# A two-layer block on one core: modulation tiles in pairs at the start, inputs 0 to 511 first, and pooling matmuls one chunk later

## The chip, the cores and the metric

The kernel runs on one core of a Trainium2 chip. The time is the device time of one execution, in microseconds (us); three runs of the kernel before gave 3119.91 to 3122.59, median 3122.0. One more execution was profiled, and all rows below are of that one.

Engine names as in the profile: PE is TensorE (PEld its weight loads), DVE VectorE, ACT ScalarE, POOL GpSimd, SP the engine that here issues every DMA, in order.

## The reference

Two streams of 256 tokens and 1024 features go through the block: x (the output) and ctx. There are twelve sublayers, s = 0 to 11: eight feed-forward ones (0, 2, 3, 5, 6, 8, 9, 11) and four mixers (1 differential attention, 4 neighbourhood attention, 7 pooling with grouped attention, 10 convolution with a state-space part). Sublayers 0 to 3 and parts of 4 are done for both streams. In sublayers 0 to 5 the input is normalised and modulated, and the output is gated:

```
mx = (silu(c) @ ada_w[i] + ada_b[i])        # nine vectors of 1024 for each layer i, for x
mc = (silu(c_ctx) @ ada_w[i] + ada_b[i])    # the same weights, for ctx
u  = rmsnorm(h) * g_pre * (1 + scale) + shift
a, b = split(u @ w_in, 2)
h  = h + 0.5 * gate * rmsnorm(silu(a) * b @ w_out) * g_post
```

For sublayer 0, shift is vector 0, scale vector 1, gate vector 2. Mixer 7 projects u to a pooling part (256 wide), queries, keys and values; the pooling part is averaged over windows of 2, 4, 8 and 16 tokens minus itself (a product with a constant matrix), goes through a small weight `pool_w`, and is scaled; rotated queries and keys go through attention with a window mask and a sink; both results are projected together.

## The kernel before

**Weights in slots.** All large weights (439 slots of 1 MB and one small one) pass through a ring of three raw buffers. `load_slot(g)` (L299) is an SP DMA that waits until slot g - 3 is split. `make_high` (L316, the operation at L326) rounds the slot on ACT, `make_rest` (L328, L336) forms the remainder on DVE. `highs(upto)` and `rests(upto)` advance these. Each product is three matmuls (`three`, L347; L349 to L351): high by high, high by rest, rest by high. `LEAD` = 2: ACT and DVE split two slots ahead of the one that PE is at.

**A feed-forward sublayer.** Its first product has 11 feature pairs f, each with two slots: half 0 holds inputs 0 to 511 of 256 + 256 output columns (the a and b parts), half 1 inputs 512 to 1023. `half_of(f, half, tt)` in `ffn_in_pe` does one slot for 128 tokens tt: 12 matmuls of 512 columns. Then ACT takes the silu (`silu_act`), DVE the product (`gate_dve`, L732), PE turns it (`turn_gate`, L712), ACT and DVE split it. The second product has 11 slots (`out_pe`). From sublayer 5 on (`exposed`) PE does the first halves of features 0 and 1 before the second ones.

**Modulation.** A vector of 1024 is eight tiles of 128 rows by 1024. `load_ada` (L365, the DMA at L368) brings a tile of 0.5 MB into a ring of three (`ADA_RING`) after the tile three before it was used; `sum_ada` (L383) multiplies it on DVE by `silu(cond)` and sums the rows, once for each stream; `take_mod` (L396 to L403) adds the bias and forms scale, shift or gate. `ada_plan` (L107) spreads the tiles over the slots: vector 1 for both streams and vector 0 for x before the first slot, the rest one tile a spot beside slots. A gate is stored to memory by `store_post_mod` (L421) and read back as a row by `load_post_gain` (L434), both in SP's order.

**The opening.** SP loads cond (both streams), the parameters, three modulation tiles, the identity, the tokens of x, then 13 more tiles with slots 0 to 2 between them, then the ctx tokens. ACT takes silu of cond and a small exponential for mixer 1 (`attention_setup_act`, L1736, with `attention_setup_dve`, L1724 to L1732), then the mean square (L542) and root (L549) of the tokens. DVE forms 24 sums, and normalises (L574). PE turns the normalised rows (L587). ACT applies scale and shift (L605) and rounds (L610), DVE forms the rest (L620). This is done for tokens 0 to 127, and after that for 128 to 255, through one buffer `xn`. PE's first weight matmul waits for both and for slot 0.

**Mixer 7.** `Even.pe` runs six projection chunks. After chunk 1 it waits for the constants (`ev_const`, `ev_rope`, `ev_pool_w`, loaded by SP once chunk 1 is done), then pools (L1649); after chunk 2 come the products with `pool_w` (L1657), after chunks 3 to 5 the rotations (L1209). ACT copies the pooled rows (L1689) between the copies of its chunks.

Of the kernel before, what the change touches and what calls it, by code (L numbers as in the profile page):

```python
# [56 lines left out]

PASSES = [(0, 0), (0, 1), (1, 0), (1, 1), (2, 0), (2, 1), (3, 0), (3, 1)] + [(s, 0) for s in range(4, 12)]
# [75 lines left out]
def build_program(nc, t, out):  # L134
# [3 lines left out]
    for name, src, row, n, cols in plan:  # L138
        first[name], count_of[name] = len(slot_cols), n
        slot_cols += [cols] * n  # L140
        source += [(src, row + j) for j in range(n)]
# [9 lines left out]
    with ExitStack() as ctx:  # L151
# [48 lines left out]
        gt = place("gated", [P, 2, 2, SEQ], F32, offset=mix_at + 69632)  # L200
        ada_terms = place("ada_terms", [P, D], F32, offset=mix_at + 73728)
# [23 lines left out]
        cond_landed = sem("cond_landed")  # L225
# [130 lines left out]
        pre_mods = [(0, 1, (0, 1)), (0, 0, (0,)), (0, 0, (1,)), (0, 3, (0, 1)), (0, 4, (0, 1)), (0, 6, (0, 1)),  # L356
# [4 lines left out]
        def sums_to(n):  # L361
            return sum(len(a[4]) for a in ada[:n + 1])

        def load_ada(sp, n):
# [3 lines left out]
            sp.dma_start(ada_w[:, n % ADA_RING], t["w_ada"][(layer * N_MOD + m) * KT + kt])\  # L368
                .then_inc(ada_landed[n % ADA_RING], 16)

        def sum_ada(n):
# [3 lines left out]
            if n == 0:  # L375
                dve.wait_ge(cond_ready, 1)
            if n == first_after_da:
                dve.wait_ge(cond_ready, 2)
            before = sums_to(n - 1)
            for i, c in enumerate(conds):  # L380
                if before + i:
                    dve.wait_ge(ada_used, before + i)
                dve.tensor_tensor_reduce(ada_terms[:], ada_w[:, n % ADA_RING], cond[:, c], 1.0, 0.0, ALU.mult,  # L383
# [171 lines left out]
        def stat_dve(s, c, tt):  # L555
# [7 lines left out]
            if e:  # L563
# [7 lines left out]
            for half in range(2):  # L571
                dst, src = xn[:, HALF[half]], h[:, 2 * c + tt, HALF[half]]
# [5 lines left out]
                ins.then_inc(xn_ready, 1)  # L578

        def turn_pe(s, c, tt):  # L580
            pe = nc.tensor
            e = pre_event(s, c, tt)
            for half in range(2):
                pe.wait_ge(xn_ready, 2 * e + half + 1)
                for k in range(4):
                    kt = 4 * half + k
                    ins = pe.transpose(u_pair(s, c, tt)[:, half, k * P:(k + 1) * P], xn[:, kt * P:(kt + 1) * P], ident[:])  # L587
# [34 lines left out]

        def await_u(eng, s, c, tt):
# [19 lines left out]

        def gates_before(s, c):
# [6 lines left out]
        def ffn_in_pe(s, c):  # L651
# [3 lines left out]
            def half_of(f, half, tt):  # L655
                g = g0 + 2 * f + half
                await_rest(pe, g)
                if half == 0:
                    if f >= 2:
                        pe.wait_ge(gate_done, b0 + 2 * (f - 2) + tt + 1)  # L660
                    if f == 0 and not exposed(s):
# [24 lines left out]
            if exposed(s):  # L686
# [3 lines left out]
                for f, half in ((0, 0), (0, 1), (1, 0)):  # L690
                    half_of(f, half, 1)
            for f in range(NF):
                for half in range(2):
                    if exposed(s) and (f, half) < (1, 1):
                        continue
                    for tt in range(2):
                        half_of(f, half, tt)
                    if half == (f == 1 and exposed(s)) and f:
# [16 lines left out]
        def silu_act(s, c, f, tt):  # L715
# [4 lines left out]
            else:  # L720
                act.wait_ge(w_used, first[f"in{s}{'xc'[c]}"] + 2 * f + 2)
# [91 lines left out]
        def ffn_act(s, c):  # L813
            act = nc.scalar
            g0, g1 = first[f"in{s}{'xc'[c]}"], first[f"out{s}{'xc'[c]}"]
            for f in range(NF):
                highs(g0 + 2 * f + LEAD)
                if f == 0:
# [6 lines left out]
                    if (s, c) == (2, 0):  # L825
                        silu_cond(2)
                if f and not (exposed(s) and f == 1):
                    ghi_act(s, c, f - 1)
                highs(g0 + 2 * f + 1 + LEAD)
                silu_act(s, c, f, 0)  # L830
                silu_act(s, c, f, 1)
                if exposed(s) and f == 1:
# [21 lines left out]
        def ffn_dve(s, c):  # L854
            g0, g1 = first[f"in{s}{'xc'[c]}"], first[f"out{s}{'xc'[c]}"]
            for f in range(NF):
# [4 lines left out]
                if f and not (exposed(s) and f == 1):  # L861
                    glo_dve(s, c, f - 1)
                rests(g0 + 2 * f + 1 + LEAD)
                gate_dve(s, c, f, 0)
                gate_dve(s, c, f, 1)
                if exposed(s) and f == 1:
# [355 lines left out]
        class DiffAttention:  # L1222
# [64 lines left out]
            def act(self, act):  # L1287
                g0 = self.proj.g0
                for c in range(16):
# [10 lines left out]
                    ctx_act(1, c)  # L1300
                self.attend_act()
# [4 lines left out]
            def dve(self, dve):  # L1306
                g0 = self.proj.g0
                for c in range(16):
                    rests(g0 + c + LEAD)
                    ctx_dve(1, c)  # L1310
                    sums_at(g0 + c)
# [1212 lines left out]
```

## Time and profile before

| | |
|---|---|
| median of 3 runs | 3122.0 us (3119.91 to 3122.59) |
| profiled execution | 3125.98 us, span 3124.2 us, mean granted clock 0.969 |
| PE busy | 2922.5 us, 94% |
| DVE busy | 2024.0 us, 65% |
| ACT busy | 1462.8 us, 47% |
| HBM read | 563.50 MB, 181 GB/s over the span |

The span runs from the first to the last instruction. Matmuls are pipelined, so one of 0.39 us follows another after less than that; distances between starts are what counts. A row's last part in square brackets is how long its engine sat idle before it, and what ended that. The clock is the granted share of 2.4 GHz: 1.00, or 0.50 for 1.2 GHz.

### The profile page before, as it was taken

How to read it: one execution, taken by the hardware profiler on the slowest of the kernel's cores; microseconds unless marked ns; L12 is line 12 of the kernel's file. 1: busy time of each engine (PE TensorE's matmuls, PEld its weight loads, DVE VectorE, ACT ScalarE, POOL GpSimd, SP SyncE). 2: the span in 40 equal slices, each digit the busy share in tenths (PEclk: the TensorE clock that was granted, in tenths of full speed). 3: DMA queues.
4: the chain of work that ended last, by engine and by line, in shares of the span. 5: the costliest groups of instructions: out<-in, count | busy, mean ns of one | idle time of the engine just before them, and what ended most of it. 6: DMA issues, size and time to landing. Idle time of an engine off the chain costs nothing.

```text
span 3124.2 us, 36463 instructions
## 1 busy us (share of the span) xinstructions
PE 2922.5 (94%) x14132; PEld 2393.6 (77%) x14132; DVE 2024.0 (65%) x2650; ACT 1462.8 (47%) x2164; POOL 168.2 (5%) x162
## 2 busy tenths in 40 slices
PE   2999999989999999999899999998999999878999
PEld 1887878757888888788885787887578788876787
DVE  6778785576788787855536555545665554597654
ACT  3445453475454454545535544444444444444543
POOL 0000000000000000000400000000000000393000
PEclk9999999999999999999999999999599999889999
DMA  7767674206677778965530455554055455430453
GB/s 268 247 222 291 229 237 145 88 1 231 214 277 248 233 270 247 307 205 187 218 115 1 163 187 175 202 189 158 13 182 183 173 202 189 147 121 14 158 185 135
DMA packets 101547, 566.96 MB, mean 181 GB/s; under 512 B 20480, under 2 KB 20992, under 8 KB 44672
## 3 DMA queue, kind: packets, MB, share of 16 engines
q1 hardware_dynamic: 101376, 564.63, 52.4%
q8 instruction: 114, 1.87, 0.2%
q14 instruction: 57, 0.47, 0.0%
HBM read 563.50 MB, written 1.09 MB: 181 GB/s over the span
## 4 chain that ended last, share of the span: by engine, by line
PE 80%; DVE 10%; ACT 4%; DMA 3%; issue 3%; SPq 0%; DVEq 0%; ACTq 0%
PE banks L349 23%; PE banks L351 22%; PE banks L350 22%; DVE ada_terms L383 2%; PE banks L1093 2%; DVE w_rest L336 2%; PE banks L1112 2%; PE banks L712 2%; ACT w_high L326 1%; PE banks L1101 1%; DVE od_glu L1805 1%; DVE od_xbc L1846 1%; DMA w_raw<-in_w_ffn_out 1%; DMA post_mod<-post_scale 1%; DMA ada_tiles<-in_w_ada 1%
## 5 line engine op out<-in xcount | busy, mean ns | idle before, releaser
L336 DVE TENSOR_TENSOR w_rest<-w_raw,w_high 128x2048 fp32r<-128x2048 f32 x426 | 978.8, 2299 | 560.7 <-ACT w_high L326 560.5
L326 ACT ACTIVATE w_high<-w_raw 128x2048 fp32r<-128x2048 f32 x426 | 811.1, 1907 | 236.7 <-PE banks L351 211.2
L349 PE MATMUL banks<-w_high,u_parts 128*128 128x512 f32 (+1 forms) x2160 | 828.5, 384 | 23.6 <-DVE post_term L490 13.9
L351 PE MATMUL banks<-w_high,u_parts 128*128 128x512 f32 (+1 forms) x2160 | 817.0, 378 | 0.0
L350 PE MATMUL banks<-w_rest,u_parts 128*128 128x512 f32 (+1 forms) x2160 | 815.5, 378 | 0.0
L349 PEld LDWEIGHTS banks<-w_high,u_parts 128*128 128x128 f32 x2160 | 410.8, 190 | 97.0 <-issue 26.2
L351 PEld LDWEIGHTS banks<-w_high,u_parts 128*128 128x128 f32 x2160 | 410.3, 190 | 76.0
L350 PEld LDWEIGHTS banks<-w_rest,u_parts 128*128 128x128 f32 x2160 | 411.2, 190 | 70.9
L349 PE MATMUL banks<-w_high,gated_high 128*128 128x512 f32 x968 | 379.3, 392 | 4.4 <-DVE w_rest L336 3.1
L351 PE MATMUL banks<-w_high,gated_rest 128*128 128x512 f32 x968 | 376.9, 389 | 0.0
L350 PE MATMUL banks<-w_rest,gated_high 128*128 128x512 f32 x968 | 376.8, 389 | 0.0
L383 DVE CUSTOM_DVE_ANT_0 ada_terms<-ada_tiles,cond_rows 128x1024 f32<-128x1024 f32 x256 | 312.8, 1222 | 22.0 <-DMA ada_tiles<-in_w_ada 14.8
L739 ACT ACTIVATE gated_high<-banks 128x512 fp32r<-128x512 f32 x121 | 72.5, 599 | 419.6 <-PE banks L712 419.3
L724 ACT ACTIVATE silu_out<-banks 128x256 f32<-128x256 f32 x242 | 91.9, 383 | 308.2 <-PE banks L351 294.6
L349 PEld LDWEIGHTS banks<-w_high,gated_high 128*128 128x128 f32 x968 | 181.8, 188 | 43.4 <-DVE w_rest L336 6.0
L351 PEld LDWEIGHTS banks<-w_high,gated_rest 128*128 128x128 f32 x968 | 181.7, 188 | 37.9
L350 PEld LDWEIGHTS banks<-w_rest,gated_high 128*128 128x128 f32 x968 | 181.8, 188 | 36.9
L349 PE MATMUL banks<-u_parts,w_high 128*128 128x256 f32 (+1 forms) x544 | 180.7, 332 | 14.2 <-DVE w_rest L336 14.2
L350 PE MATMUL banks<-u_parts,w_high 128*128 128x256 f32 (+1 forms) x544 | 177.8, 327 | 0.0
L351 PE MATMUL banks<-u_parts,w_rest 128*128 128x256 f32 (+1 forms) x544 | 177.7, 327 | 0.0
L746 DVE TENSOR_TENSOR gated_rest<-banks,gated_high 128x512 fp32r<-128x512 f32 x121 | 83.3, 689 | 126.9 <-ACT gated_high L739 126.9
L732 DVE TENSOR_TENSOR gated<-silu_out,banks 128x256 f32<-128x256 f32 x242 | 99.7, 416 | 93.5 <-ACT silu_out L724 93.5
(243 smaller groups left out, 2950.1 us busy)
## 6 DMA issues: line engine op xcount, KB each, us to landing
w_raw<-in_w_ffn_in SPq DMA_DIRECT2D x242, 1024.0 KB, 5.0
w_raw<-in_w_ffn_out SPq DMA_DIRECT2D x121, 1024.0 KB, 5.0
ada_tiles<-in_w_ada SPq DMA_DIRECT2D x152, 512.0 KB, 5.5
w_raw<-in_w_mix SPq DMA_DIRECT2D x54, 1024.0 KB, 5.0
w_raw<-in_w_mix_out SPq DMA_DIRECT2D x22, 1024.0 KB, 5.0
post_gain_row<-post_mod SPq DMA_DIRECT2D x10, 512.0 KB, 6.2
na_bias<-in_na_bias SPq DMA_DIRECT2D x1, 4096.0 KB, 14.2
pre_gain_row<-in_gain SPq DMA_DIRECT2D x6, 512.0 KB, 8.4
```

The lines of the kernel that those rows point to most:

```text
L326: act.activation(w_high(g)[:, 0:n], raw[:, g % RING, 0:n], ACT.Copy).then_inc(w_hi_ready, 1)
L336: nc.vector.tensor_tensor(w_rest(g)[:, 0:n], raw[:, g % RING, 0:n], w_high(g)[:, 0:n].bitcast(F32), ALU.subtract).then_inc(w_lo_ready, 1)
L349: nc.tensor.matmul(ps, hi_a, hi_b, start=first_, stop=False)
L350: nc.tensor.matmul(ps, hi_a, lo_b, start=False, stop=False)
L351: return nc.tensor.matmul(ps, lo_a, hi_b, start=False, stop=last_)
L383: dve.tensor_tensor_reduce(ada_terms[:], ada_w[:, n % ADA_RING], cond[:, c], 1.0, 0.0, ALU.mult, ALU.add, mod_sum[:, layer * N_MOD + m, c, ...
L712: ins = pe.transpose(ps[:, o:o + P], gt[:, f % 2, tt, k * P:(k + 1) * P], ident[:])
L724: act.activation(fa[:, f % 2, tt], bank[in_bank(s, f, tt)][:, 0:SEQ], ACT.Silu).then_inc(silu_done, 1)
L732: dve.tensor_tensor(gt[:, f % 2, tt], fa[:, f % 2, tt], bank[in_bank(s, f, tt)][:, SEQ:], ALU.mult)\
L739: act.activation(ghi[:, 2 * f:2 * f + 2].rearrange("p a n -> p (a n)"), bank[4 + f % 2], ACT.Copy)\
L746: dve.tensor_tensor(glo[:, 2 * f:2 * f + 2].rearrange("p a n -> p (a n)"), bank[4 + f % 2], ghi[:, 2 * f:2 * f + 2].rearrange("p a n -> p ...
L1093: pe.matmul(bank[m % 4][:, 0:it["keys"]], q, k, start=True, stop=True)\
```

## The change

1. The opening. The 16 tiles of vectors 1 and 0 come as eight transfers of two tiles (1 MB each), every one into a place of its own in memory that later holds gated activations, the ctx part of `u`, or the tile ring. Their order is vector 1 tiles 0 to 3, vector 0 tiles 0 to 3, then tiles 4 to 7 of both. cond is loaded and goes through silu in two halves. All 16 are first summed for x alone.
2. Halves of 512 features. `take_first`, `first_part_act`, `first_shift_dve` and `first_part_dve` work on inputs 0 to 511 for all tokens and then on 512 to 1023. ACT does the normalising; ACT and DVE share scale and shift by tokens; tokens 128 to 255 use `t1` as a second buffer.
3. Sublayer 0 of x takes its slots in the order (f, half) = (0, 0), (1, 0), (0, 1), (1, 1), and the load order is changed to match. ACT's silu and DVE's products of feature 0 move to feature 1.
4. The 16 ctx sums of the same tiles go into DVE's features 0 to 5 (3, 3, 3, 3, 3, 1). Later tiles move two places on, the last two to the ctx value chunks of mixer 1.
5. `attention_setup` moves from the opening to chunk 3 of mixer 1.
6. Mixer 7: the pooling matmuls move behind chunk 2, those with `pool_w` behind chunk 3 and ahead of that chunk's rotations; ACT's and DVE's parts move along.

```
+FIRST_PAIRS = [(1, 0), (1, 2), (0, 0), (0, 2), (1, 4), (1, 6), (0, 4), (0, 6)]
+FIRST_CTX = [[14, 15, 0], [5, 1, 6], [7, 2, 8], [3, 9, 4], [10, 11, 12], [13]]
...
-    tiles = [(-1, *u) for u in ada_units(0, 1, (0, 1)) + ada_units(0, 0, (0,))]
-    late = ada_units(0, 0, (1,))
-    units = [late[2 * n:2 * n + 2] for n in range(4)]
+    tiles, units = [], []
...
-    spots = [first["in0x"] + 2 * f for f in range(NF)] + [first["out0x"] + j for j in range(NF)]
+    spots = [first["in0x"] + 2 * f for f in range(6, NF)] + [first["out0x"] + j for j in range(NF)]
     spots += [first["in0c"] + 2 * f for f in range(NF)] + [first["out0c"] + j for j in range(NF)]
-    spots += [first["qk1"] + j for j in range(8)]
+    spots += [first["qk1"] + j for j in range(8)] + [first["v1c"] + j for j in range(2)]
...
+        order = [0, 2, 1, 3] + list(range(4, n)) if name == "in0x" else range(n)
+        source += [(src, row + j) for j in order]
...
+        def take_first(half):
+            dve = nc.vector
+            kts = slice(4 * half, 4 * half + 4)
+            dve.wait_ge(ada_used, 8 * half + 8)
+            dve.tensor_tensor(B[:, 0, 0, kts], mod_sum[:, 0, 0, kts], pcol("ada_b", 4 * half, 4 * half + 4), ALU.add)
+            link(dve, dve.tensor_tensor(mod_sum[:, 1, 0, kts], mod_sum[:, 1, 0, kts],
+                                        pcol("ada_b", KT + 4 * half, KT + 4 * half + 4), ALU.add))
+            dve.scalar_tensor_tensor(A[:, 0, 0, kts], mod_sum[:, 1, 0, kts], 1.0,
+                                     pcol("gain", 4 * half, 4 * half + 4), ALU.add, ALU.mult)\
+                .then_inc(first_mod_ready, 1)
...
+        def first_normed_act(tt):
+            ...
+            for half in range(2):
+                act.activation(normed(e)[:, HALF[half]], h[:, tt, HALF[half]], ACT.Identity,
+                               scale=pre_col[:, 4, e:e + 1]).then_inc(xn_ready, 1)
...
+        def first_part_act(half):
+            act = nc.scalar
+            act.wait_ge(xn_turned, half + 1)
+            act.wait_ge(first_mod_ready, half + 1)
+            for k in range(4):
+                kt = 4 * half + k
+                ins = act.activation(first_cols(0)[:, kt], turned(0, 0, 0, half)[:, k], ACT.Identity,
+                                     scale=A[:, 0, 0, kt:kt + 1], bias=B[:, 0, 0, kt:kt + 1])
+            ins.then_inc(v_ready, 1)
+            act.wait_ge(v_ready, 2 * half + 2)
+            for tt in range(2):
+                act.activation(u[:, 0, 0, 4 * half:4 * half + 4, tt * P:(tt + 1) * P],
+                               first_cols(tt)[:, 4 * half:4 * half + 4], ACT.Copy).then_inc(uhi_ready, 1)
...
+        def first_shift_dve(half):
+            ...
+            for k in range(4):
+                ins = dve.tensor_scalar(first_cols(1)[:, kt], turned(0, 0, 1, half)[:, k], A[:, 0, 0, kt:kt + 1],
+                                        B[:, 0, 0, kt:kt + 1], ALU.mult, ALU.add)
...
+        def first_part_dve(half):
+            ...
+            for tt in range(2):
+                dve.wait_ge(uhi_ready, 2 * half + tt + 1)
+                dve.tensor_tensor(u[:, 0, 1, kts, cols], first_cols(tt)[:, kts],
+                                  u[:, 0, 0, kts, cols].bitcast(F32), ALU.subtract).then_inc(u_ready, 1)
...
+                if (s, c) == (0, 0) and f == 0:
+                    pe.wait_ge(u_ready, 2 * half + tt + 1)
...
+            if (s, c) == (0, 0):
+                for f, half in ((0, 0), (1, 0), (0, 1)):
+                    for tt in range(2):
+                        half_of(f, half, tt)
...
+                if (s, c) == (0, 0) and f < len(FIRST_CTX):
+                    sums_of_ctx(f)
...
@@ Even.pe
-                    if c == 1:
+                    if c == 2:
                         pe.wait_ge(const_landed, 16 * self.const)
...
-                    if c == 2:
+                    if c == 3:
                         pe.wait_ge(self.taken, 2)
...
@@ block.sync
+            load_cond(sp, 0)
+            load_first(sp, 0)
+            load_first(sp, 1)
+            sp.dma_start(h[:, 0:2], t["tokens"][0:2].rearrange("a p d -> p a d")).then_inc(in_landed[0], 16)
             sp.dma_start(par[:], t["params"]).then_inc(par_landed, 16)
             sp.dma_start(ident[:], t["identity"]).then_inc(par_landed, 16)
+            load_first(sp, 2)
+            load_slot(sp, 0)
+            load_first(sp, 3)
+            load_first(sp, 4)
+            load_slot(sp, 1)
+            load_first(sp, 5)
+            load_first(sp, 6)
+            load_first(sp, 7)
+            load_slot(sp, 2)
+            load_cond(sp, 1)
...
@@ block.vector
+            dve.wait_ge(cond_ready, 1)
+            for n in range(4):
+                sum_first(n, 0, n)
+            first_stat_dve(0)
+            first_stat_dve(1)
+            for n in range(4, 8):
+                sum_first(n, 0, n)
             dve.wait_ge(par_landed, 32)
+            take_first(0)
+            first_shift_dve(0)
+            rests(0)
+            first_part_dve(0)
+            for n in range(8, 16):
+                sum_first(n, 0, n)
+                if n == 11:
+                    rests(1)
+            take_first(1)
+            first_shift_dve(1)
+            rests(2)
+            first_part_dve(1)
+            dve.wait_ge(cond_ready, 2)
             ffn_dve(0, 0)
```

## Rows read from the trace of the kernel before

**Rows 1.** Waits of PE, whole run: what waited, for what, us in total, times, longest.
```profile
PE banks L587 <- DVE normed L574: 63.7, 7, 29.5
PE banks L1649 <- DMA ev_pool_w<-in_pool_w: 6.6, 1, 6.6
```

**Rows 2.** Timeline of the opening: start, duration (us), engine, line, operation, idle before.
```profile
5.56 1.28 ACT L2172 ACT_TABLE_LOAD   x1 [5.56 <-DMA cond_rows<-in_cond]
6.86 1.91 ACT L2172 ACTIVATE cond_rows<-cond_rows 128x2048 f32<-128x2048 f32 x1
...
12.52 1.22 DVE L383 CUSTOM_DVE_ANT_0 ada_terms<-ada_tiles,cond_rows 128x1024 f32<-128x1024 f32 x1
13.38 0.63 ACT L542 ACTIVATE squares_unread<-residual 128x512 bf16<-128x512 f32 x1 [1.66 <-DMA residual<-in_tokens]
...
13.79 1.22 DVE L383 CUSTOM_DVE_ANT_0 ada_terms<-ada_tiles,cond_rows 128x1024 f32<-128x1024 f32 x1
...
36.50 8.05 SPq L368 DMA_DIRECT2D ada_tiles<-in_w_ada  x4
...
46.86 2.29 DVE L336 TENSOR_TENSOR w_rest<-w_raw,w_high 128x2048 fp32r<-128x2048 f32 x1
...
53.12 1.50 ACT L605 ACTIVATE normed<-banks,pre_shift,pre_scale 128x128 f32<-128x128 f32 x4 [22.05 <-DVE pre_shift L396]
...
55.31 0.69 DVE L620 TENSOR_TENSOR u_parts<-normed,u_parts 128x512 fp32r<-128x512 f32 x1 [2.29 <-ACT u_parts L610]
...
66.13 0.77 PE L349 MATMUL banks<-w_high,u_parts 128*128 128x512 f32 x1 [4.27 <-DVE u_parts L620]
...
71.39 0.47 PE L349 MATMUL banks<-w_high,u_parts 128*128 128x512 f32 x1
```

**Rows 3.** Stretch 8 to 12 us: length, PE, PEld, DVE, ACT, POOL busy, clock, DMA share, GB/s.
```profile
8.00:12.00 4.00, 0.00 (x0) 0.00 (x0) 0.68 (x6) 2.25 (x3) 0.00 (x0) 1.00 1.03 415
```

**Rows 4.** Chain of waits, first gate transpose of sublayer 0: start, duration, what.
```profile
85.26 0.44 PE banks L712 x4
```

**Rows 5.** Stretch 100 to 150 us, columns as in rows 3.
```profile
100.00:150.00 50.00, 50.00 (x230) 41.40 (x229) 35.98 (x40) 22.14 (x23) 0.00 (x0) 1.00 0.72 251
```

**Rows 6.** Timeline of SP at the first stored gate.
```profile
208.60 1.06 SPq L421 DMA_DIRECT2D post_mod<-post_scale  x2
221.34 0.33 SPq L434 DMA_DIRECT2D post_gain_row<-post_mod  x1
```

**Rows 7.** Timeline of DVE, ctx value chunks of mixer 1.
```profile
589.57 2.29 DVE L336 TENSOR_TENSOR w_rest<-w_raw,w_high 128x2048 fp32r<-128x2048 f32 x1 [3.69 <-ACT w_high L326]
```

**Rows 8.** Timeline of mixer 7; the row of a DMA alone is from the chain.
```profile
2149.02 2.29 DVE L336 TENSOR_TENSOR w_rest<-w_raw,w_high 128x2048 fp32r<-128x2048 f32 x1 [8.13 <-ACT w_high L326]
...
2149.17 0.28 PE L350 MATMUL banks<-w_rest_lead,u_parts 128*128 128x256 f32 x1
2149.29 0.28 PE L351 MATMUL banks<-w_high_lead,u_parts 128*128 128x256 f32 x1
2150.45 5.64 DMA ev_pool_w<-in_pool_w
2156.13 3.74 PE L1649 MATMUL banks<-ev_const,ev_u 128*64 128x256 f32 x16 [6.56 <-DMA ev_pool_w<-in_pool_w]
...
2186.15 1.03 PE L1209 MATMUL banks<-ev_qk,ev_rope 128*128 128x256 f32 x4
```

**Rows 9.** Stretch 2156 to 2160 us, the pooling matmuls, columns as in rows 3.
```profile
2156.00:2160.00 4.00, 3.87 (x17) 2.09 (x18) 0.00 (x0) 0.48 (x2) 0.00 (x0) 0.50 1.01 426
```

**Rows 10.** Groups by line in 2196 to 2256 us (mixer 7's attention): one per item.
```profile
L1163 DVE TENSOR_TENSOR banks<-banks,ev_const 128x256 f32<-128x256 f32 x22 | 9.5, 432 | 17.0 <-PE banks L1093 17.0
```

**Rows 11.** Stretch 2208 to 2220 us, columns as in rows 3.
```profile
2208.00:2220.00 12.00, 12.00 (x36) 6.47 (x35) 8.06 (x33) 5.33 (x22) 0.00 (x0) 0.50 0.01 1
```

**Rows 12.** Neighbourhood attention: a stretch of 50 us, and its items in 1640 to 1712 us.
```profile
1650.00:1700.00 50.00, 50.00 (x265) 29.22 (x263) 36.16 (x95) 27.65 (x75) 0.00 (x0) 1.00 0.00 1
...
L1163 DVE TENSOR_TENSOR banks<-banks,na_bias 128x256 f32<-128x256 f32 x27 | 11.7, 432 | 17.9 <-PE banks L1093 17.9
```

More of the change, by code:

```diff
@@ L361, in sums_to, with ada_slot, load_first, sum_first @@
         def sums_to(n):
-            return sum(len(a[4]) for a in ada[:n + 1])
+            return 4 * len(FIRST_PAIRS) + sum(len(a[4]) for a in ada[:n + 1])
+        def ada_slot(n):
+            return (n + 2) % ADA_RING
+        def load_first(sp, q):
+            m, kt = FIRST_PAIRS[q]
+            sp.dma_start(first_tiles[q][:], t["w_ada"][m * KT + kt:m * KT + kt + 2].rearrange("a p d -> p a d"))\
+                .then_inc(first_landed[q], 16)
+        def sum_first(tile, c, n):
+            dve = nc.vector
+            q, i = tile // 2, tile % 2
+            m, kt = FIRST_PAIRS[q]
+            dve.wait_ge(first_landed[q], 16)
+            if n:
+                dve.wait_ge(ada_used, n)
+            dve.tensor_tensor_reduce(ada_terms[:], first_tiles[q][:, i], cond[:, c], 1.0, 0.0, ALU.mult, ALU.add,
+                                     mod_sum[:, m, c, kt + i:kt + i + 1]).then_inc(ada_used, 1)
+        def take_first(half):
+            dve = nc.vector
+            kts = slice(4 * half, 4 * half + 4)
[6 more added lines that the diff above has]
+                .then_inc(first_mod_ready, 1)
+        def sums_of_ctx(f):
+            done = 2 * len(FIRST_PAIRS) + sum(len(tiles) for tiles in FIRST_CTX[:f])
+            for i, tile in enumerate(FIRST_CTX[f]):
+                sum_first(tile, 1, done + i)
+            if f == len(FIRST_CTX) - 1:
+                take_mod(0, 1, (1,), -1)
+                take_mod(0, 0, (1,), -1)
         def load_ada(sp, n):
@@ L642, in in_bank, with pairs_first, slot_in @@
             return tt + 2 * (f % 2) if not exposed(s) else 2 * tt + f % 2
+        def pairs_first(s, c):
+            return exposed(s) or (s, c) == (0, 0)
+        def slot_in(s, c, f, half):
+            g = first[f"in{s}{'xc'[c]}"]
+            return g + 2 * half + f if (s, c) == (0, 0) and f < 2 else g + 2 * f + half
         def gates_before(s, c):
@@ L660, in half_of @@
                         pe.wait_ge(gate_done, b0 + 2 * (f - 2) + tt + 1)
-                    if f == 0 and not exposed(s):
+                    if f == 0 and not exposed(s) and (s, c) != (0, 0):
                         await_u(pe, s, c, 1)
@@ L697, in ffn_in_pe @@
                         half_of(f, half, tt)
-                    if half == (f == 1 and exposed(s)) and f:
+                    if half == (f == 1 and pairs_first(s, c)) and f:
                         turn_gate(s, c, f - 1)
@@ L720, in silu_act @@
             else:
[L721 removed]
+                act.wait_ge(w_used, slot_in(s, c, f, 1) + 1)
             if f >= 2:
@@ L2184, in build_program @@
             else:
-                spot = max(ada[n - ADA_RING][0] + AHEAD, RING)
+                spot = first["in0x"] + 8 if n < ADA_RING else ada[n - ADA_RING][0] + AHEAD
             ada_after.setdefault(spot, []).append(n)
```

147 lines of the change are left out of this document (88 added, 59 removed).

## Prediction

> **What bounds the kernel now.** I began with the waits of PE over the whole run: the transposes at L587 wait 63.7 us for DVE's normalised rows, nearly all of it before the first projection, and the pooling matmuls at L1649 wait 6.6 us once for a transfer [rows 1]. These are the two places that the change touches, so I read the opening next, as a timeline [rows 2]. PE's first weight matmul starts at 66.13. Until then DVE forms 24 row sums at 1.27 us each (the distance of the first two), waits for tiles because SP can't issue a load before one of three buffers is free (the row at 36.50 holds 8.05 us for four loads), and only at 53.12 has ScalarE the shift and scale, after 22.05 us of waiting. The DMA engines are not the limit there on average: when loads are queued they move 415 GB/s [rows 3]. Behind the opening, PE is busy 50.00 of 50 us with DVE at 35.98 [rows 5], so each us by which that stretch starts earlier is a us of the total, unless a later stall gives it back. Last I read mixer 7 around 2150 [rows 8, 9].
>
> **The opening, step by step.** I date the new order by rows of before. *Landing:* cond (1.05 MB) is there at 5.56, and the tokens at 13.38 with 4.15 MB queued up to and including them [rows 2]; a straight line, 3.0 us plus 0.40 MB per us, fits both. The new SP order has no ring wait, and each 1 MB adds 2.6 us: cond of x 4.3, pairs 0 and 1 at 6.9 and 9.6, tokens 12.2, params and identity 13.4, pair 2 16.0, slot 0 18.6, pair 3 21.3, pair 4 23.9, slot 1 26.5, pairs 5 to 7 29.1, 31.8, 34.3, slot 2 37.0, cond of ctx 38.3, the ctx tokens 41.0, slot 3 43.5.
> *DVE, first half:* sums of tiles 0 to 3 lie under the landing and under squares and roots, which ScalarE does between 12.2 and 15.7. Normalising moves to ScalarE: not seen there on this shape, I bound it by 0.5 to 0.8 us for each 512 columns (its square of the same shape takes 0.63) and hide it, since the transposes are done near 19. Tiles 4 and 5 take 16.0 to 18.6, tiles 6 and 7 21.3 to 23.9. take_first is three tiny operations, 0.8. The four shifted copies out of PSUM on DVE have no row: their 512 columns are at least the 0.69 of L620's and at most ScalarE's 1.50 for four [rows 2]; I take 1.0, nearer the DVE row, 25.7. rests(0) 2.29 gives 28.0, and the first low part 0.69 gives **28.7, where PE starts**, against 66.13.
> *PE:* it now takes inputs 0 to 511 of feature pairs 0 and 1 first (slots 0 and 1 in the new load order), then 512 to 1023 (slots 2 and 3). In before the first 12 matmuls of 512 columns took 5.26 us (66.13 to 71.39), the next 60 until the gate transpose 13.87, 0.231 each [rows 2, 4]. Slot 0 is done at 36.8.
> *DVE, second half:* from 29.4 tiles 8 to 11, 34.6; rests(1) 36.9, so slot 1 runs on PE until 42.5; tiles 12 to 15, 42.1; take 42.9; copies 43.9; rests(2) 46.2; low part 46.9. PE idles 4.4 us there and begins slot 2 at 46.9. The bound in this stretch is DVE, no longer the loads.
> *Hand-over:* ScalarE needs the u copies to 45.7, a table load 1.28 and half of cond's 1.91, so DVE's new wait for cond_ready 2 ends at 48.0 and not 47.6; all of the FFN's DVE work stands behind it. Three ctx sums 51.9, rests(3) and (4) 56.4, three sums 60.3, rests(5) 62.6, two gate products 63.5. Slot 3 starts on PE when rests(3) is done, 54.2, and ends by 60; the transpose then waits for the gates, so slot 4 starts at **64.0**. In before, slot 4 starts after the first gate transpose at 85.26 [rows 4], its 0.44 and slot 3's 24 matmuls (5.6): 91.3. **The term is 27.3 us.** A slow clock at slot 2 costs 12 times 0.21, 2.5 us, more on PE, which the wait for the gates hides.
> *Bounds:* if the loads run at the 251 GB/s of the steady stage [rows 5], pair 3 lands at 32, PE starts near 39.5, pair 7 lands at 53, slot 2 starts at 60 and slot 4, by the same 17 us between them, at 77: a term of 14; if DVE's copies cost 0.7 and the gates are not last, slot 4 could start at 60, a term of 31.
>
> **What lies behind it.** In features 0 to 5 DVE has 16 ctx sums where it had 12 others; per feature pair that is two rests (4.6), two products (0.8), one low part (0.7) and three sums (3.8), 9.9 us under PE's 11.3: nothing, with 1.4 us of cover; without it 0.1 to 1.4 us per pair. All later modulation tiles move two units later. The store of the first gate moves from beside slot 6 of the FFN's second product to beside slot 8; SP is held 11.7 us by it (208.60, next issue 221.34) [rows 6] with three loaded slots ahead. It then meets the dense DVE stretch 11 us later: I count 0, and keep -1 to +4. Four ctx sums land in the ctx value chunks of mixer 1, where DVE waits 3.69 us for a slot anyway [rows 7]: 0, at most 1. The lambda set-up (eight small operations, about 1.5 us) leaves the opening, where it stood before the first sum, and goes to a chunk with two slots prepared: its gain is inside the dates above, its cost there 0 to 0.5.
>
> The trace moves 415 GB/s with loads of half a MB already queued [rows 3], so pairs of 1 MB are booked with no better rate. The Trainium skill (DMA: Bandwidth & Descriptors, Bandwidth) gives 341 GB/s for transfers of 1 MB and asks for that size. By its rate, an estimate from that page, pair 3 would land 3.1 us later and the time be 3 us above my sum; no row here supports the lower rate.
>
> **Mixer 7.** Chunk 1 ends at 2149.5, its matmuls 0.12 us apart. PE then waits 6.56 us for pool_w, landed at 2156.1, and runs 16 pooling matmuls in 3.74 us [rows 8] with a clock of 0.50 [rows 9]. Moved behind chunk 2, whose slot DVE split before the one of 2149.02, the wait holds chunk 2's 48 matmuls at 0.12 us (2149.5 to 2155.3); 0.8 us are left, the clock has no reason to fall, and the pooling takes half, 1.9. Saved: 6.6 - 0.8 + 1.8 = 7.6, and 0.5 for the slow first matmuls of chunk 2: **8.1 us**. Queued behind the wait is chunk 3, whose slot is ready at 2151.3 [rows 8]. ScalarE no longer holds the split of chunk 4's slot behind the pooling copies. The second pooling matmuls and the rotations only change places. The rotation behind chunk 5, at 2186.15 in before, comes near 2178 of the same clock. Late next is chunk 5's slot, loaded behind the constants: at 0.40 MB per us 2.8 MB from 2149.6 on land by 2160, and it is wanted at 2171. Bounds: 5.8 (pooling stays cold) and 8.5.
>
> **Sum.** 27.3 + 8.1 = 35.4 off the profiled span of 3124.2 (execution 3125.98, so 3090.6). The runs' median, 3122.0, lies 4.0 below that execution, and I predict from it: 3122.0 - 35.4 = 3086.6, **3087**.
>
> **Rivals.**
> *The loads or DVE are later than dated.* For: the copies and the ScalarE normalising are unseen, and 14 transfers queued at once may finish out of order. Against: pool_w came 5.64 us after its issue with 1.7 MB up to it and four transfers behind it, as a queue in order gives. Opening 19 instead of 27 (halfway towards the slow bound), or less of it, or the store's stall unhidden by 4, or both: 3122.0 - 19 - 4 - 8 gives **3091 to 3101**, middle 3096.
> *Mixer 7's attention runs at full clock.* It now takes 60 / 22 = 2.73 us per item [rows 10] with PE busy 12.00 of 12 us and the clock at 0.50 [rows 11], so it is PE at half speed that sets it; at full speed DVE's 8.06 of 12 us (1.9 us per item) would. 24 items times 0.7 is 17 us, **3070**. For: the stretch before it is rearranged. Against: the last rotations and scores, the gaps ahead of the attention, are as before, and the runs shown agree within 3 us. The Trainium skill (TensorE: Matmul & The Clock Gate, What's actually happening) says that sustained activity lifts the clock; by that rule this stretch would not stay slow, and the trace does not follow it for 60 us.
> *The neighbourhood attention falls to half clock instead.* This is the slower case. It is PE-bound at full speed, 72 / 27 = 2.67 us per item, PE busy 50.00 of 50 [rows 12], with the same small products as mixer 7's. Its 32 items would take 85 us more: 3087 + 85 = **3172**. It decides if more than 13 of the 32 items run slow, since 35.4 / 2.67 is 13. For: mixer 7 shows such a state. Against: nothing near it is changed but its date.
> *The change does nothing in the opening* (PE idles later for what it did early): only mixer 7's 8 us, 3114; DVE's 36 us of 50 against it [rows 5].
>
> **How the numbers follow.** Forecast 0.66 (own range 3079 to 3092), later loads 0.17, full clock in mixer 7 0.08, opening given back 0.04, slower 0.05 with whatever else of that kind. The range 3073 to 3100 leaves out the last cases, half of the fast case and the tail of the late one. A measurement of this kernel can tell 0.2% (6 us) from no change: faster 0.94, same 0.01, slower 0.05.
>
> **What would show it.** First weight matmul at 28 to 30; an idle PE of 4 to 5 us before slot 2; the first gate transpose of feature 0 at 63 to 64; features from there at 11.3 us; the end of that stage 27 us earlier, and the start of mixer 7 too. There the pooling matmuls at 0.12 us each under a clock of 1.00, wait below 1 us. Wrong if PE starts after 33, if it idles again before feature 5, if SP's hold at the store shows as an idle PE above 3 us, or if either attention changes its clock.

## The result, and the profile after

| | before | after |
|---|---|---|
| median of 4 runs each, side by side | 3121.48 us (3119.91 to 3122.59) | 3089.58 us (3086.59 to 3092.31) |
| ratio, 95% interval | | 0.9898 (0.9881 to 0.9915) |
| profiled execution, its span, mean clock | 3125.98, 3124.2, 0.969 | 3090.01, 3087.8, 0.969 |

The medians are 31.9 us apart, the profiled spans 36.4. The forecast was 3087 us, range 3073 to 3100, faster 0.94: it holds. Of the sum of 35.4 us about 30 to 32 came, though, and its terms were not hit equally well, so the terms are what is worth reading.

The waits of PE over the whole run, with the columns of [rows 1]. The line numbers have moved: L587 is now L658, L574 is L623 and L1649 is L1784.

```profile
PE banks L658 <- ACT normed L644: 17.2, 1, 17.2
...
PE banks L359 <- DVE u_parts L729: 13.1, 2, 8.7
...
PE banks L658 <- DVE normed L623: 4.6, 5, 1.3
...
PE banks L1784 <- DMA ev_pool_w<-in_pool_w: 2.0, 1, 2.0
```

The 63.7 us of [rows 1] have become 17.2 + 4.6 = 21.8: in the opening one wait of 17.2 for ScalarE, which normalises there now, instead of two of 29.5 and 28.5 for DVE, and 4.6 at the same transposes later on. A further 18.0 us at these transposes, for another DVE line, are the same in both kernels. The first matmuls of either half wait 13.1 for the low parts. The 6.6 us for `pool_w` are 2.0.

The timeline of the opening, to be held against [rows 2]:

```profile
5.12 1.06 ACT L2310 ACTIVATE cond_rows<-cond_rows 128x1024 f32<-128x1024 f32 x1 [2.91 <-DMA cond_rows<-in_cond]
...
8.17 1.23 DVE L390 CUSTOM_DVE_ANT_0 ada_terms<-ada_first,cond_rows 128x1024 f32<-128x1024 f32 x1 [7.15 <-DMA ada_first<-in_w_ada]
...
22.02 1.23 DVE L390 CUSTOM_DVE_ANT_0 ada_terms<-ada_first,cond_rows 128x1024 f32<-128x1024 f32 x1 [2.46 <-DMA ada_first<-in_w_ada]
...
25.27 1.36 DVE L720 TENSOR_SCALAR post_term<-banks,pre_scale,pre_shift 128x128 f32<-128x128 f32 x4
26.56 2.28 DVE L346 TENSOR_TENSOR w_rest<-w_raw,w_high 128x2048 fp32r<-128x2048 f32 x1
28.75 0.69 DVE L729 TENSOR_TENSOR u_parts<-normed,u_parts 128x512 fp32r<-128x512 f32 x1
...
29.59 0.76 PE L359 MATMUL banks<-w_high,u_parts 128*128 128x512 f32 x1 [8.70 <-DVE u_parts L729]
...
47.69 0.76 PE L359 MATMUL banks<-w_high,u_parts 128*128 128x512 f32 x1 [4.37 <-DVE u_parts L729]
...
48.45 1.23 DVE L390 CUSTOM_DVE_ANT_0 ada_terms<-ada_tiles,cond_rows 128x1024 f32<-128x1024 f32 x1 [0.31 <-ACT cond_rows L2310]
...
52.36 4.49 DVE L346 TENSOR_TENSOR w_rest<-w_raw,w_high 128x2048 fp32r<-128x2048 f32 x2
...
62.87 1.41 DVE L855 TENSOR_TENSOR gated<-silu_out,banks 128x256 f32<-128x256 f32 x4
...
63.67 1.12 PE L835 MATMUL banks<-identity,gated 128*128 128x128 f32 x4 [2.23 <-DVE gated L855]
```

First matmul 29.59 (dated 28.7), slot 2 47.69 with 4.37 of idle before it (46.9, 4.4), DVE's wait for the silu of the context over at 48.45 (48.0), gates from 62.87 on (62.6), transpose 63.67, slot 4 at 64.44 (64.0).

The first stored gate, SP and DVE, to be held against [rows 6], and the pooling of mixer 7 with its transfer (a row of the chain), against [rows 8]:

```profile
196.58 1.06 SPq L470 DMA_DIRECT2D post_mod<-post_scale  x2
208.67 0.33 SPq L483 DMA_DIRECT2D post_gain_row<-post_mod  x1
209.04 0.43 SPq L314 DMA_DIRECT2D w_raw<-in_w_ffn_out  x1
...
217.75 2.29 DVE L346 TENSOR_TENSOR w_rest<-w_raw,w_high 128x2048 fp32r<-128x2048 f32 x1 [4.23 <-ACT w_high L336]
...
220.10 0.50 PE L359 MATMUL banks<-w_high,gated_high 128*128 128x512 f32 x1 [0.72 <-DVE w_rest L346]
224.71 0.50 PE L359 MATMUL banks<-w_high,gated_high 128*128 128x512 f32 x1 [1.59 <-DVE w_rest L346]
...
2123.24 6.88 DMA ev_pool_w<-in_pool_w
2130.16 2.00 PE L1784 MATMUL banks<-ev_const,ev_u 128*64 128x256 f32 x16 [2.04 <-DMA ev_pool_w<-in_pool_w]
```

Stretches of after, columns as in [rows 3]; the second answers to [rows 5], the third to [rows 9], the fourth to [rows 11], the last to [rows 12]:

```profile
8.00:12.00 4.00, 0.00 (x0) 0.00 (x0) 3.54 (x5) 0.00 (x0) 0.00 (x0) 1.00 1.02 419
100.00:150.00 50.00, 50.00 (x230) 41.35 (x229) 35.50 (x41) 22.11 (x22) 0.00 (x0) 1.00 0.63 221
2130.00:2132.00 2.00, 1.83 (x16) 1.22 (x16) 0.00 (x0) 0.38 (x1) 0.00 (x0) 1.00 0.99 418
2208.00:2220.00 12.00, 12.00 (x36) 6.48 (x35) 8.06 (x33) 5.33 (x22) 0.00 (x0) 0.50 0.01 1
1650.00:1700.00 50.00, 48.97 (x267) 31.34 (x266) 32.59 (x82) 28.07 (x69) 0.00 (x0) 1.00 0.00 1
```

Neither attention changed its clock: mixer 7's is still at 0.50, the neighbourhood one at 1.00.

How far after lies ahead of before at the same instruction, from the two timelines:

| place | before | after | ahead |
|---|---|---|---|
| a gate transpose late in the first input product | 198.67 | 173.40 | 25.3 |
| first gate transpose of the next pass | 274.44 | 251.64 | 22.8 |
| transposes at the head of mixer 7 | 2138.21 | 2113.57 | 24.6 |
| first scores of mixer 7's attention | 2192.53 | 2158.76 | 33.8 |
| end of the span | 3124.2 | 3087.8 | 36.4 |

So 25.3 in the opening, 2.5 lost around the stored gate, 1.8 won back between there and mixer 7, 9.1 in mixer 7 and 2.6 behind it, where nothing was changed. The experiments ask which of these are the change's.

### The profile page after: what moved, and what is told of

It is laid out like the page before. It is cut to its first block, busy times and chain, and to the rows that moved or that the text cites. A ratio compares the mean times of both kernels' runs of the same rounds, so it can differ in the third digit from the quotient of the medians.

```text
span 3087.8 us, 36466 instructions
## 1 busy us (share of the span) xinstructions
PE 2922.6 (95%) x14132; PEld 2393.4 (78%) x14132; DVE 2024.4 (66%) x2657; ACT 1462.2 (47%) x2163; POOL 168.8 (5%) x162
## 4 chain that ended last, share of the span: by engine, by line
PE 81%; DVE 9%; ACT 4%; DMA 3%; issue 3%; SPq 0%; DVEq 0%; ACTq 0%
PE banks L359 23%; PE banks L361 23%; PE banks L360 23%; PE banks L1229 2%; PE banks L1248 2%; PE banks L835 2%; DVE w_rest L346 2%; ACT w_high L336 1%; PE banks L1237 1%; DVE od_glu L1943 1%; DVE od_xbc L1984 1%; DMA ada_tiles<-in_w_ada 1%; DMA post_mod<-post_scale 1%; PE banks L2288 1%; DVE ada_terms L432 1%
## 5 line engine op out<-in xcount | busy, mean ns | idle before, releaser
L359 PEld LDWEIGHTS banks<-w_high,u_parts 128*128 128x128 f32 x2160 | 411.7, 191 | 107.1 <-issue 21.8
L432 DVE CUSTOM_DVE_ANT_0 ada_terms<-ada_tiles,cond_rows 128x1024 f32<-128x1024 f32 x224 | 273.7, 1222 | 14.8 <-DMA ada_tiles<-in_w_ada 9.9
```

The costliest lines, as they stand in the source:

```text
L359: nc.tensor.matmul(ps, hi_a, hi_b, start=first_, stop=False)
L432: dve.tensor_tensor_reduce(ada_terms[:], ada_w[:, ada_slot(n)], cond[:, c], 1.0, 0.0, ALU.mult, ALU.add, mod_sum[:, layer * N_MOD + m, c, ...
```

## Experiments

They were run in three groups, each on another chip and each beside runs of the kernel before. Single times scatter by 3 us and more to each side, so effects of a few us are read from the dates in the profiles; none of the small variants of the changed kernel can be told from it by its time.

**The changed kernel again.** No edit.

> The changed kernel once more, as the measure for the three beside it. Theory (the opening gives 25.3 us, mixer 7 gives 6.8 us, the store of the gains takes back 2.4 us in between, and the rest of the 36.4 us between the two profiled spans is the granted clock at the head of mixer 7, about 2.4 us): 31 to 34 us under the kernel before, in a profile first matmul at 29.6, first gate turn at 63.7, end of the first input halves 25.3 us earlier than before. Rival (the 36.4 us are all structure): 36 us under it.

Measured: 3089.96 against 3119.66, ratio 0.9902 (0.9885 to 0.9919), 29.7 us; span 3087.0. The dates of the opening repeat to 0.02 us (first matmul 29.58, transpose 63.66). The next gate transpose is at 69.62 where the first profile has 71.15:

```profile
63.66 0.66 PE L835 MATMUL banks<-identity,gated 128*128 128x128 f32 x4 [3.24 <-DVE gated L855]
69.62 0.60 PE L835 MATMUL banks<-identity,gated 128*128 128x128 f32 x4
```

The transpose takes 0.66 here and 1.12 above. The stretch behind it, columns as in [rows 3], first profile and then this one:

```profile
64.00:68.00 4.00, 4.00 (x15) 3.31 (x14) 1.71 (x3) 2.40 (x2) 0.00 (x0) 0.63 0.91 339
64.00:68.00 4.00, 4.00 (x20) 3.35 (x19) 2.16 (x3) 2.40 (x2) 0.00 (x0) 1.00 0.91 338
```

It began at the lower clock in one execution and not in the other, and that is the 1.5 us between the two, still there at the end of the first input product (173.40 and 171.84). Of the eleven profiles with the new opening four have it. The 29.7 us are just under the 31 to 34 of the theory, which lie inside the interval (25 to 36 us), with the rival's 36 at its edge. What speaks against that rival is the second profile of the kernel before (below), 8.2 us shorter than the first.

**The opening alone.** In the class of mixer 7 the pooling matmuls stay where they were:

```
-                    if c == 2:
+                    if c == 1:
                         pe.wait_ge(const_landed, 16 * self.const)
```

> The opening as changed, the attention of mixer 7 as before. Theory: the opening alone is worth 25.3 us up to the end of the first input part and about 24 us at the end, so 24 to 25 us under the kernel before and 6.8 us above the changed one; the pooling matmuls of mixer 7 stand behind the 6.6 us DMA wait again. Rival (opening as predicted, 27.3 us): 27 us under. Rival (the early gain is given back later, because the shift changes what collides with what): under 20 us.

**Mixer 7 alone.** The reverse: the kernel before with the pooling at `c == 2` and the second product at `c == 3`.

> The opening as before, only the pooling matmuls of mixer 7 one chunk further on. Theory: 6.8 us under the kernel before (6.6 us wait gone and the slow pooling of 3.7 us run in 2.0, less a new wait of 2.0), in the profile a wait of 1 to 2 us before the first pooling matmul; 9 us if the clock of the chunks 0 and 1 is full, 6 to 7 if it is not. Rival (the prediction's term): 8.1 us with 0.8 us of idle left. Rival (the attention behind it runs at full clock): 17 us.

Measured: opening alone 3098.52, ratio 0.9929 (0.9914 to 0.9945), 21.1 us under before and 8.6 above the changed kernel; mixer 7 alone 3111.13, ratio 0.9970 (0.9961 to 0.9979), 8.5 us under. The two make 29.6, and together they gave 29.7: within the intervals (17 to 27 us for the opening, 7 to 12 for mixer 7) the parts add. The theory for the opening, 24 to 25, and its rival of 27 lie inside or at the edge of that interval; by date the opening alone is 25.2 us ahead at the end of the first input product (173.45 against 198.67). For mixer 7 the time can't tell 6.8 from 8.1; the wait left, 2.05, is near the theory's 1 to 2 and not the 0.8 of the prediction, and the rival of 17 us falls. With the pooling in its old place the old wait is back, on the shifted dates:

```profile
2131.05 3.73 PE L1789 MATMUL banks<-ev_const,ev_u 128*64 128x256 f32 x16 [6.48 <-DMA ev_pool_w<-in_pool_w]
```

Mixer 7 alone has the new one:

```profile
2155.18 2.00 PE L1644 MATMUL banks<-ev_const,ev_u 128*64 128x256 f32 x16 [2.05 <-DMA ev_pool_w<-in_pool_w]
```

**Both halves awaited.** The first matmuls wait for features 512 to 1023 as well; loads, sums and ScalarE's part stay new.

```
-                    pe.wait_ge(u_ready, 2 * half + tt + 1)
+                    pe.wait_ge(u_ready, 2 + tt + 1)
```

> The changed kernel, but the first input matmuls wait for the features 512 to 1023 too, so that slots 0 and 1 no longer run while the second half is summed. Theory (the part of the opening that is due to the order of the features): first matmul at 47.5 instead of 29.6, four slots of 5.8 us behind one another end near 72, slot 4 starts at 73 to 74 instead of 64.8: 8 to 9 us above the changed kernel. Rival (slot 4 is bound by VectorE's sums for the context and the gates, so the early slots are hidden anyway): 0 to 2 us above it. Rival (an engine that waits longer also gets a slower clock): 11 to 13 us above.

Measured: 3098.22, ratio 0.9929 (0.9915 to 0.9944), 8.3 us above the changed kernel.

```profile
47.73 0.77 PE L359 MATMUL banks<-w_high,u_parts 128*128 128x512 f32 x1 [26.80 <-DVE u_parts L729]
...
72.09 0.66 PE L835 MATMUL banks<-identity,gated 128*128 128x128 f32 x4 [0.28 <-DVE gated L855]
```

The gate transpose comes 8.4 us later, and the wait before it is down to 0.28: PE, and hardly DVE, is the late one, as the theory said. Features 0 to 511 first is thus worth 8.3 us; the other 13 to 18 us of the opening come from loads without a ring wait and from the sums and ScalarE's normalising in their new order, which were not taken apart further.

**Single tiles.** The pair loads are halved, same places, same order, a semaphore for each tile:

```
-            sp.dma_start(first_tiles[q][:], t["w_ada"][m * KT + kt:m * KT + kt + 2].rearrange("a p d -> p a d"))\
-                .then_inc(first_landed[q], 16)
+            for i in range(2):
+                sp.dma_start(first_tiles[q][:, i], t["w_ada"][m * KT + kt + i]).then_inc(first_landed[2 * q + i], 16)
```

> The changed kernel with the sixteen modulation tiles loaded one by one (0.5 MB each, a semaphore each) into the same places and in the same order. Theory (what brings the opening is the order and the earlier issue, not the size of a load): first matmul within 1 us of 29.6, slot 4 starts within 1.5 us of 64.8, time within 2 us of the changed kernel. Rival (pairs are what brings it, since SyncE issues half as many loads before it is held): with 24 loads instead of 16 ahead of slot 2 the last modulation tile and slot 2 land 3 us later or more, and the time is 3 us or more above it.

Measured: 3086.95 (before 3118.35), ratio 0.9904 (0.9890 to 0.9917).

```profile
6.62 1.23 DVE L390 CUSTOM_DVE_ANT_0 ada_terms<-ada_first,cond_rows 128x1024 f32<-128x1024 f32 x1 [5.61 <-DMA ada_first<-in_w_ada]
...
20.46 1.23 DVE L390 CUSTOM_DVE_ANT_0 ada_terms<-ada_first,cond_rows 128x1024 f32<-128x1024 f32 x1 [1.49 <-DMA ada_first<-in_w_ada]
...
28.03 0.77 PE L359 MATMUL banks<-w_high,u_parts 128*128 128x512 f32 x1 [7.42 <-DVE u_parts L729]
```

Neither had this sign, though the time is within 2 us of the changed kernel's as the theory said: everything from the first matmul to the first gate transpose (62.12) is 1.5 us earlier. Tile 6 is summed from 20.46 on and not from 22.02, since it no longer waits for its partner. The pairs bring nothing by themselves; by date they cost 1.5 us.

**Gains loaded later.** Loads of a gain that wait for its store stand three slots behind the store:

```
-            gain_after.setdefault(max(g + AHEAD, store_spot.get(s, 0)), []).append((s, c))
+            gain_after.setdefault(max(g + AHEAD, store_spot.get(s, -3) + 3), []).append((s, c))
```

> The changed kernel with every load of a post-norm gain that waits for a store put three slots behind the store instead of directly behind it. Theory (the 2.4 us lost between 207 and 252 us are SyncE waiting for the 11.6 us store of the gains with the next weight slot queued behind it): the PE waits of 0.7 and 1.6 us near 220 to 225 us are gone, the shift against the kernel before stays 25.2 us across 250 us, and the time is 2 to 2.5 us less than the changed kernel's. Rival (the slots there are late because the sums on VectorE run late, not because of the store): the waits stay and the time is the same.

Measured: 3086.62, ratio 0.9910 (0.9895 to 0.9924). SP now goes on behind the store:

```profile
196.64 1.06 SPq L470 DMA_DIRECT2D post_mod<-post_scale  x2
198.47 2.31 SPq L314 DMA_DIRECT2D w_raw<-in_w_ffn_out  x1
...
212.78 0.43 SPq L483 DMA_DIRECT2D post_gain_row<-post_mod  x1
```

Both PE waits at 220 and 225 are gone, and the gate transpose of the next pass is at 249.26 against 251.64, with the same date (71.25 against 71.15) at the gate transpose of feature 1. That is the stall of the store, as the theory said. From the last gate transpose of the first input product to this one it is 77.9 to 78.3 us in the nine profiles with the new opening and the load in its place, 75.8 here and 76.5 in the run with all edits; the three profiles with the old opening have 75.8, 76.2 and 77.0. So the stall costs 0.9 to 2.5 us. The gain of 2 to 2.5 us in the time is not shown. Another 6 us of this profile's span lie scattered between 250 and 2105, where it also has the least time at the clock of 0.50 of all profiles (34 us, the others 38 to 55); the run with all edits has the same change and not these, so they are not counted.

**Context sums one feature later.**

```
-FIRST_CTX = [[14, 15, 0], [5, 1, 6], [7, 2, 8], [3, 9, 4], [10, 11, 12], [13]]
+FIRST_CTX = [[], [14, 15, 0, 5], [1, 6, 7], [2, 8, 3], [9, 4, 10], [11, 12, 13]]
```

> The changed kernel with the sums for the context begun one feature later (none, then 4, 3, 3, 3, 3 tiles instead of 3, 3, 3, 3, 3, 1). Theory (slot 4 waits for the gates of feature 0, and these stand behind six context sums of 1.3 us on VectorE): the three sums ahead of them go, less the one that feature 1 gains, so the gates come 2.6 us earlier, the PE wait before the first gate turn (2.2 to 3.2 us) is gone, with it the slow clock behind it, and slot 4 starts at 61.5 to 62.5: 2.2 to 3.5 us under the changed kernel. Rival (the wait only moves on, because the sums that come later delay the gates of features 1 to 4): gone by the end of the first input part, same time.

Measured: 3089.67, ratio 0.9908 (0.9894 to 0.9921); the gate transpose is at 63.07, 0.6 us earlier and not 2.6, and PE still waits 2.81 before it. The theory falls; of the rival, that it is all gone by the end of the first input product, the 0.6 left there (172.84 against 173.40) says as little as the time. The three sums had covered a wait:

```profile
50.38 4.49 DVE L346 TENSOR_TENSOR w_rest<-w_raw,w_high 128x2048 fp32r<-128x2048 f32 x2 [2.27 <-ACT w_high L336]
```

**The same, and the high half of slot 3 made early.** In ScalarE's program `highs(2)` ahead of `first_part_act(1)` becomes `highs(3)`.

> The changed kernel with the context sums begun one feature later, as in the run before, and with ScalarE making the high half of slot 3 before it shifts the second half of the features, so that VectorE finds it at 48. Theory (in the run with the later sums VectorE waited 2.3 us for the high half of slot 3, at 48.1 to 50.4, which the three sums had covered): that wait is gone, the gates of feature 0 come near 60, the first gate turn at 60.5 to 61.2 instead of 63.7 with under 1 us of PE idle before it, the end of the first input part 2.5 to 3.5 us earlier than in the changed kernel, and the time 2.5 to 3.5 us below it. Rival (the high half of slot 3 then delays the shift of the second half of the features, and slot 2 with it): slot 2 starts after 48.5, no gain.

Measured: 3087.75, ratio 0.9902 (0.9884 to 0.9920). The theory falls and the rival's mechanism holds, at 48.36 and not the 48.5 it named: slot 3 had not landed, ScalarE waited for it, and the shift and slot 2 behind it came 0.7 us later. The gate transpose is at 63.10, where the run before had it.

```profile
43.52 1.91 ACT L336 ACTIVATE w_high<-w_raw 128x2048 fp32r<-128x2048 f32 x1 [4.39 <-DMA w_raw<-in_w_ffn_in]
```

**Pair 3 before slot 0.** The two loads change places in SP's order.

> The changed kernel with the load of pair 3 issued before that of weight slot 0. Theory (the sums of the first half end behind pair 3, which lands at 22.0, and slot 0 is needed only behind them): pair 3 lands near 19.5 and slot 0 near 22, the first matmul comes 1.5 to 2.5 us earlier than 29.6; slot 4 is bound by the gates behind VectorE's sums, which also move up, unless slot 0's split stands in their way: 0.5 to 2 us under the changed kernel. Rival (slot 0's rest, made at 26.6, then becomes the late one): first matmul at 29.6 or later, same time or 1 us above.

Measured: 3085.97, ratio 0.9901 (0.9884 to 0.9918). First matmul 27.28, 2.3 us earlier, slot 2 45.39, gate transpose 61.36, all by the same 2.3: the theory holds by date. The 0.5 to 2 us in the time can't be seen; the runs lie between 3081.7 and 3096.7. A load in the wrong place at 5 us is still there at 61.

**All four.** Single tiles, pair 3 first, gains later, context sums later with the early high half.

> The changed kernel with what helped, all together: single tiles, pair 3 before slot 0, gains stored without holding the slots, context sums one feature later with the high half of slot 3 made early. If the gains add (1.6 and 2.3 us at the first matmul, of which some 2.7 together since VectorE then sums without a break; 2.4 us at the store; 3 us at the first gate turn): first matmul near 26.9, first gate turn near 58, 8 us below the changed kernel, 3081 to 3083 us. Rival (the same slack is counted twice, VectorE's busy time is the bound of the opening): 4 to 5 us below it.

Measured: 3085.35 against 3118.75, ratio 0.9888 (0.9868 to 0.9908). The first matmul is at 26.83 as expected, but slot 2 starts at 48.45:

```profile
48.45 0.76 PE L359 MATMUL banks<-w_high,u_parts 128*128 128x512 f32 x1 [7.89 <-DVE u_parts L729]
```

The early high half of slot 3 took nearly all that the first two had gained: ScalarE waits 4.63 us for that slot and the gate transpose is at 63.19, not near 58. Neither the 8 us nor the rival's 4 to 5 can be confirmed by the time. No version here is shown faster than the changed kernel by its time: all intervals overlap. The combination without that edit and without the later sums was not run.

**The kernel before, and the opening alone, once more.** One profile of each.

> The kernel before once more, for its profile. Theory (without the move of the pooling matmuls the chunks 0 and 1 of mixer 7 run at half clock, with it at full clock: so far 2 of 2 against 8 of 8 profiles): granted clock 0.50 for some 5 us from the first matmul after the turn at 2138 to 2141 on, and the profiled span near 3119 to 3124. Rival (chance): full clock there.

> The opening as changed, mixer 7 as before, once more for its profile. Theory as for the kernel before: clock 0.50 over chunks 0 and 1 of mixer 7 (2116 to 2122). Rival (chance): full clock there.

The same five us at the head of mixer 7 (chunks 0 and 1), columns as in [rows 3]. The kernel before, first profile:

```profile
2141.00:2146.00 5.00, 4.97 (x23) 5.00 (x24) 0.00 (x0) 0.67 (x2) 0.00 (x0) 0.50 0.00 0
```

The kernel before, second profile (3117.79 us, span 3116.0):

```profile
2140.00:2145.00 5.00, 4.65 (x39) 4.68 (x40) 0.20 (x1) 2.49 (x5) 0.00 (x0) 1.00 0.00 0
```

39 matmuls against 23 in the same time, with the same instructions. The opening alone (3099.8) was at 0.50 there again. Context sums later with the early high half, which has the pooling moved:

```profile
2115.00:2120.00 5.00, 4.98 (x23) 5.00 (x24) 0.00 (x0) 0.65 (x2) 0.00 (x0) 0.50 0.00 0
```

So the theory, that the move decides this clock, falls on both sides, though it held for the opening alone. What does decide it is open: the two profiles of the kernel before differ in it with the same program. From the transposes at the head to the first scores it takes:

| | clock 0.50 in chunks 0 and 1 | 1.00 there |
|---|---|---|
| pooling in its old place | 54.3, 54.3, 54.2 | 51.3 |
| pooling moved | 47.7, 47.8 | 45.2 to 45.3 (4 profiles), 45.6, 46.7 to 46.9 (3) |

Down a column, like with like, the move is worth 4.4 to 6.7 us, most often 6.0 to 6.7; three of ten profiles with the move had the lower clock in the pooling itself (3.0 to 3.2 us and not 2.0), which makes the 46.7 to 46.9.

## Why the prediction was right, and where its terms were off

- **PE start, 28.7; measured 29.59.** The landings came 0.7 to 1.3 us later than dated (pair 0 8.17 against 6.9, pair 3 22.02 against 21.3), and DVE's four shifted copies took 1.36 and not 1.0. A sum takes 1.37 from start to start and not the 1.27 read from the first two of before. The straight line of landings held: 419 GB/s at 8 to 12 us.
- **Slot 2, the context wait, the gates.** Within 0.8 us, the idle of 4.4 to 0.03. That DVE, no longer the loads, bounds this stretch is right. In front of the first matmul the loads still bound: DVE idled 2.46 us for pair 3, as the dates had it (18.6 to 21.3), and one load moved ahead gave 2.3 us.
- **"A slow clock at slot 2 costs 2.5 us, which the wait for the gates hides": right, but not the last.** The slow stretch came again behind the wait at the gate transpose, where nothing hides it: 1.5 us in one of the two profiles of the changed kernel. The term of 27.3 measures 25.3 and 26.8 (198.67 less 173.40 and 171.84). Besides this stretch it missed 0.4 on the one side, the transpose ahead of slot 4 (64.44, not 64.0), and 0.3 on the other (slot 4 of before starts at 91.0, not 91.3).
- **"I count 0" for the store: the step that failed.** It was kept between -1 and +4 and cost 0.9 to 2.5 us, 2.5 in the two first profiles. SP is held 11.0 us, much as before (11.7), but the three loaded slots did not last: DVE then idles 4.23 us at 217.75, and PE waits 0.72 and 1.59. In before the same idle was shorter, and the first PE wait behind it is 0.49, at 247.8:

```profile
230.40 2.29 DVE L336 TENSOR_TENSOR w_rest<-w_raw,w_high 128x2048 fp32r<-128x2048 f32 x1 [2.82 <-ACT w_high L326]
```

  Moving the gain's load removes both waits, which shows the cause.
- **Mixer 7, 8.1; measured 6.0 to 6.7 where the clocks are alike, 4.4 with a slow pooling.** The mechanism is right: chunk 2 fills the wait, the pooling runs at full clock most times. 2.0 us of wait are left and not 0.8, since `pool_w` landed 6.88 us after its issue and not 5.64; SP issues one more weight slot, at 2127, while it is under way, which could be the reason and was not tested. In the timed runs the move brought 8.5 (6.6 to 12.2) and 8.6, with the unsettled clock in it, so that these do not confirm the 8.1.
- **The rest.** Context sums beside features 0 to 5, mixer 1's chunks and the lambda set-up at 0: no new PE wait there. The 1.8 us between 252 and mixer 7 are not shown to be the change's: that stretch takes 1855.8 to 1864.5 in the fourteen profiles, and 1863.8 and 1863.2 in the kernel before alone. The 2.6 us behind mixer 7 aren't the change's: from its scores to the end the fourteen profiles take 927.1 to 931.7, and the kernel before alone 931.7 and 927.2.
- **The sum.** 35.4 less 2.4 (store), 1.3 (opening) and 1.8 (mixer 7) is 30, against 31.9, 29.7 and 29.6 measured. That the span said 36.4 is for the larger part the execution of before that was profiled: 3124.2 in the one, 3116.0 in the other. Going from the median was right, and a term of a few us can't be checked against a single span; it takes the dates on both sides of it.
- **The rivals.** Later loads or DVE: not by more than 1.3 us. The clock of mixer 7's attention: unchanged, PE busy 12.00 of 12 us at 0.50. The rule of the Trainium skill (TensorE: Matmul & The Clock Gate, What's actually happening) that sustained work lifts it is again not what this stretch shows. The price set for a full clock there was summed too low: 24 items times 0.83 (2.73 - 1.9) is 20 us, not 17. The neighbourhood attention stayed at 1.00. Undone opening: no. The other figure of the Trainium skill, 341 GB/s for transfers of 1 MB (DMA: Bandwidth & Descriptors, Bandwidth), isn't what this queue of loads shows either: 419 GB/s with pairs, and pair 3 there at 22.0, not the 24.4 of that rate; cutting them in two moved the start by the wait for the second tile.

## What to carry to other kernels

Date a new opening by landing, then by the engine that works on it, row by row: it held to 1.3 us here over 60. Look at what waits in SP's order behind a transfer that itself waits for a store, since such a hold that is nearly free at one place costs when it is moved by a few slots. Work that stands in front of a wait may be its cover, and an early instruction may wait for a load: check both the next wait and the landing before moving either.

## What the runs showed of the hardware that was not expected

- The same instructions at the same place ran at a granted clock of 0.50 in one execution and 1.00 in the next (the kernel before at 2141: 23 and 39 matmuls in 5 us). Two profiles of one kernel lie 8.2 us apart by span, 3.0 of it in mixer 7 and 4.5 behind it.
- A load of two tiles makes its first tile wait for the second: summed from 22.02 on as a pair, from 20.46 on alone.
- With many MB queued, SP's own issue is held up to some us for a load (the DMA queue's row below, of the changed kernel), though no semaphore holds it there; the loads land at the same pace all the same.

```profile
5.21 4.11 SPq L379 DMA_DIRECT2D ada_first<-in_w_ada  x2
```
